# Reordering the seams between chained products of a four-layer diffusion backbone on one NeuronCore

## What is computed

```
mod = silu(cond) @ w_mod[i] + b_mod[i]
h = rms_norm(x, g_pre) * (1 + scale) + shift
out = product(s) of the sub-layer on h
x = x + gate * rms_norm(out, g_post)
```

## Time and profile before

| | |
|---|---|
| median of 3 runs | 2044.71 us (2044.56 to 2045.04) |
| profiled execution | 2046.58 us, of which span 2044.8 us |
| TensorE clock granted, mean | 0.976 |
| busy: PE, DVE, ACT, POOL | 1935.7, 1191.7, 924.0, 713.5 us |
| DMA | 324.29 MB, 44.6% of 16 engines in the main queue |

### The profile page before, as it was taken

How to read it: one execution, slowest core, us unless ns; L and a number is a source line. 1 busy time by engine, 2 the same in 40 slices (tenths; PEclk the granted TensorE clock), 3 DMA queues, 4 the chain that set the end, 5 groups by cost and what they waited for, 6 DMA issues and landing times.

```text
span 2044.8 us, 29870 instructions
## 1 busy us (share of the span) xinstructions
PE 1935.7 (95%) x11679; PEld 1713.0 (84%) x11679; DVE 1191.7 (58%) x1789; ACT 924.0 (45%) x1566; POOL 713.5 (35%) x515
## 2 busy tenths in 40 slices
PE   6699999999998989999999998899999979899998
PEld 3589998799996767999987956899987867799986
DVE  3557761566626675777615844777724684777722
ACT  3444442554546645444424325544424444544422
POOL 0223324333335553333344722333343521333342
PEclk8799999999999989999999999999999989899999
DMA  9764346433330137533374655533365413333342
GB/s 399 319 247 135 124 164 246 169 123 124 97 134 27 48 134 305 187 125 125 116 246 172 207 155 202 211 124 124 113 240 182 174 40 114 112 128 124 124 132 72
DMA packets 80316, 324.29 MB, mean 159 GB/s; under 512 B 9009, under 2 KB 17713, under 8 KB 66609
## 3 DMA queue, kind: packets, MB, share of 16 engines
q1 hardware_dynamic: 78496, 319.42, 44.6%
q10 hardware_dynamic: 1680, 2.96, 0.4%
HBM read 317.24 MB, written 5.10 MB: 158 GB/s over the span
## 4 chain that ended last, share of the span: by engine, by line
PE 81%; DVE 7%; ACT 5%; issue 3%; POOL 2%; DMA 2%; SPq 0%; DVEq 0%; ACTq 0%; POOLq 0%
PE pair L1825 18%; PE pair L1827 17%; PE pair L1826 17%; PE pair L1861 7%; PE pair L1862 7%; PE pair L1863 7%; DVE x L1333 2%; PE pair L1982 2%; PE pair L2076 1%; DMA raw<-in_pool 1%; ACT junk L908 1%; PE pair L1796 1%; DVE wk L1324 1%; PE pair L1987 1%; PE pair L2203 1%
## 5 line engine op out<-in xcount | busy, mean ns | idle before, releaser
L752 POOL TENSOR_TENSOR w_lo<-raw,w_hi 128x512 fp32r<-128x512 f32 (+1 forms) x375 | 587.8, 1569 | 1133.2 <-ACT w_hi L880 1133.1
L1825 PE MATMUL pair<-h_hi,w_hi 128*128 128x386 f32 (+1 forms) x2008 | 687.5, 342 | 13.2 <-POOL h_lo L759 10.5
L1827 PE MATMUL pair<-h_hi,w_lo 128*128 128x386 f32 (+1 forms) x2008 | 682.6, 340 | 0.0
L1826 PE MATMUL pair<-h_lo,w_hi 128*128 128x386 f32 (+1 forms) x2008 | 682.0, 340 | 0.0
L1267 DVE TENSOR_TENSOR w_lo<-raw,w_hi 128x512 fp32r<-128x512 f32 x339 | 411.3, 1216 | 325.5 <-ACT w_hi L880 325.4
L880 ACT ACTIVATE w_hi<-raw 128x1024 fp32r<-128x1024 f32 x375 | 392.9, 1050 | 292.6 <-PE pair L1863 225.6
L1825 PEld LDWEIGHTS pair<-h_hi,w_hi 128*128 128x128 f32 (+1 forms) x2008 | 380.0, 189 | 22.2 <-POOL h_lo L759 16.7
L1826 PEld LDWEIGHTS pair<-h_lo,w_hi 128*128 128x128 f32 (+1 forms) x2008 | 380.5, 189 | 0.9
L1827 PEld LDWEIGHTS pair<-h_hi,w_lo 128*128 128x128 f32 (+1 forms) x2008 | 380.0, 189 | 0.3
L1416 DVE SCALAR_TENSOR_TENSOR acc<-pair,taps,acc 128x385 f32<-128x385 f32 x176 | 108.9, 619 | 207.4 <-ACT acc L984 207.4
L984 ACT ACTIVATE acc<-pair,taps 128x386 f32<-128x386 f32 x176 | 117.3, 666 | 224.7 <-PE pair L1827 224.7
(11 more groups left out here) (286 smaller groups left out, 2128.0 us busy)
## 6 DMA issues: line engine op xcount, KB each, us to landing
raw<-in_ffn_in SPq DMA_DIRECT2D x176, 512.0 KB, 3.5
raw<-in_ffn_out SPq DMA_DIRECT2D x88, 512.0 KB, 3.5
mod_raw<-in_w_mod SPq DMA_DIRECT2D x36, 1024.0 KB, 6.8
mod_base<-in_w_mod SPq DMA_DIRECT2D x31, 1024.0 KB, 7.1
mod_more<-in_w_mod SPq DMA_DIRECT2D x18, 1024.0 KB, 20.4
raw<-in_ssd_conv SPq DMA_DIRECT2D x32, 512.0 KB, 3.5
raw<-in_ssd_z SPq DMA_DIRECT2D x16, 512.0 KB, 3.5
raw<-in_ssd_out SPq DMA_DIRECT2D x16, 512.0 KB, 3.8
```

What stands on the lines that cost most here:

```text
L752: pool.tensor_tensor(w_lo[:, m % SLOTS, 0:w], raw[:, m % SLOTS, 0:w], w_hi[:, m % SLOTS, 0:w].bitcast(F32), ALU.subtract).then_inc(w_low_p ...
L1825: ten.matmul(to, wh, h_hi[:, k, cols], start=k == 0, stop=False, skip_group_check=True)
L1826: ten.matmul(to, wh, h_lo[:, k, cols], start=False, stop=False, skip_group_check=True)
L1827: ins = ten.matmul(to, wl, h_hi[:, k, cols], start=False, stop=k == KD - 1, skip_group_check=True)
```

## The change

1. `FILLS` for 12 pieces goes from (3, 7) to (1, 6): 1, 5 and 6 pieces in place of 3, 4 and 5.
2. In `transition`, ACT rounds chunk n only after `unit_high(t, 1)`, and chunk n+1 after `unit_high(t, 2)` with the others. `unit_high(t, 0)` now comes before `first(t, 2)`, and `unit_stage(t, 1)` before `second(t, 2)`.
3. POOL does the low part of unit 0 alone, before any weight part. DVE does all 1024 columns of unit 1, and both halves of unit 2. DVE makes the low part of chunk n after `unit_stage(t, 2)`.
4. `unit_high(t, 2)` is two copies of 512 columns, of which the first doesn't wait for DVE's part of the stage. DVE's `unit_low(t, 2)` is two subtractions.
5. PE's `in_start` waits for the first half of unit 2; the second half is waited for inside the first tile, before k = 4.
6. Seam 0 keeps the orders of ACT and DVE, but takes 3 to 5, with POOL's new order.

```diff
-FILLS = {12: (3, 7), 4: (1, 3)}
+FILLS = {12: (1, 6), 4: (1, 3)}
+        def highs_made(t, c, half=1):
+            return 4 * t + c + 1 + (half if c == 2 else 0)
+        def lows_on_dve(t, c, half=1):
+            return 4 * t + c + 1 + (half if c == 2 else 0)
+        def lows_on_pool(t):
+            return t + 1
+        def stage_free(engine, e):
+            if e >= 2:
+                t, c = divmod(e - 2, 3)
+                engine.wait_ge(h_lo_pool, lows_on_pool(t))
+                engine.wait_ge(h_lo_dve, lows_on_dve(t, c))
...
             def transition(t, n):            # POOL
-                low_to(n + 1)
                 unit_low(t, 0)
-                unit_low(t, 1)
-                low_to(n + 2)
-                unit_low(t, 2)
                 low_to(n + 4)
...
             def unit_high(t, c):             # ACT
                 act.wait_ge(stage_act, e + 1)
-                act.wait_ge(stage_dve, e + 1)
-                act.activation(h_hi[:, :, cols], stage[:, e % 2, :, :], ACT.Copy).then_inc(h_hi_ready, 1)
+                if c < 2:
...
+                else:
+                    for half in range(2):
+                        ks = slice(4 * half, 4 * half + 4)
+                        if half:
+                            act.wait_ge(stage_dve, e + 1)
+                        act.activation(h_hi[:, ks, cols], stage[:, e % 2, ks, :], ACT.Copy).then_inc(h_hi_ready, 1)
...
                 first(t, 1)                  # ACT, transition
-                round_to(n + 1)
                 unit_stage(t, 0)
                 second(t, 1)
+                unit_high(t, 0)
                 first(t, 2)
-                unit_high(t, 0)
+                unit_stage(t, 1)
                 second(t, 2)
-                unit_stage(t, 1)
                 unit_high(t, 1)
-                round_to(n + 2)
+                round_to(n + 1)
                 unit_stage(t, 2)
                 unit_high(t, 2)
                 round_to(n + 4)
...
             def unit_low(t, c):              # DVE
+                for half in range(2) if c == 2 else (1,):
+                    ks = slice(0, KD) if c == 1 else slice(4 * half, 4 * half + 4)
+                    vec.wait_ge(h_hi_ready, highs_made(t, c, half))
+                    vec.tensor_tensor(h_lo[:, ks, cols], stage[:, e % 2, ks, :], h_hi[:, ks, cols].bitcast(F32),
+                                      ALU.subtract).then_inc(h_lo_dve, 1)
...
                 unit(t, 1)                   # DVE, transition
-                low_to(n + 1)
                 weigh(t, 2)
                 residual(t, 2)
+                unit_stage(t, 1)
                 unit_low(t, 0)
-                unit_stage(t, 1)
                 unit(t, 2)
                 unit_low(t, 1)
-                low_to(n + 2)
                 unit_stage(t, 2)
+                low_to(n + 1)
                 unit_low(t, 2)
                 low_to(n + 4)
...
             def tile(to, n, w, cols, behind=None):      # PE
                 for k in range(KD):
+                    if behind is not None and k == 4:
+                        ten.wait_ge(h_lo_dve, lows_on_dve(behind, 2, 1))
...
             def in_start(t):
-                for c in range(3):
-                    unit_there(t, c)
+                ten.wait_ge(h_lo_pool, lows_on_pool(t))
+                ten.wait_ge(h_lo_dve, lows_on_dve(t, 2, 0))
```

More of the change, by code:

```diff
@@ L635, in scan_traffic @@
                     else:
-                        sp.wait_ge(h_lo_dve, event(1, 2) + 1)
+                        sp.wait_ge(h_lo_dve, lows_on_dve(1, 2))
                         sp.wait_ge(mod_used, end_pieces(1)[-1] + 1)
@@ L757, in unit_low @@
                 e, cols = event(t, c), slice(AT[c], AT[c] + P)
-                pool.wait_ge(h_hi_ready, e + 1)
+                pool.wait_ge(h_hi_ready, highs_made(t, c))
                 pool.tensor_tensor(h_lo[:, 0:4, cols], stage[:, e % 2, 0:4, :], h_hi[:, 0:4, cols].bitcast(F32),
@@ L916, in unit_stage @@
                 act.wait_ge(mod_done, vector_done(l, SHIFT1 if part else SHIFT0))
-                if e >= 2:
-                    act.wait_ge(h_lo_pool, e - 1)
-                    act.wait_ge(h_lo_dve, e - 1)
+                stage_free(act, e)
                 for k in range(4):
@@ L928, in unit_high @@
                 act.wait_ge(stage_act, e + 1)
-                act.wait_ge(stage_dve, e + 1)
-                act.activation(h_hi[:, :, cols], stage[:, e % 2, :, :], ACT.Copy).then_inc(h_hi_ready, 1)
+                if c < 2:
+                    act.wait_ge(stage_dve, e + 1)
+                    act.activation(h_hi[:, :, cols], stage[:, e % 2, :, :], ACT.Copy).then_inc(h_hi_ready, 1)
+                else:
+                    for half in range(2):
+                        ks = slice(4 * half, 4 * half + 4)
+                        if half:
+                            act.wait_ge(stage_dve, e + 1)
+                        act.activation(h_hi[:, ks, cols], stage[:, e % 2, ks, :], ACT.Copy).then_inc(h_hi_ready, 1)
             def transition0(n):
@@ L1347, in unit_stage @@
                 vec.wait_ge(mod_done, vector_done(l, SHIFT1 if part else SHIFT0))
-                if e >= 2:
-                    vec.wait_ge(h_lo_pool, e - 1)
-                    vec.wait_ge(h_lo_dve, e - 1)
+                stage_free(vec, e)
                 for k in range(4, KD):
@@ L1358, in unit_low @@
                 e, cols = event(t, c), slice(AT[c], AT[c] + P)
-                vec.wait_ge(h_hi_ready, e + 1)
-                vec.tensor_tensor(h_lo[:, 4:, cols], stage[:, e % 2, 4:, :], h_hi[:, 4:, cols].bitcast(F32),
-                                  ALU.subtract).then_inc(h_lo_dve, 1)
+                for half in range(2) if c == 2 else (1,):
[3 more added lines that the diff above has]
+                                      ALU.subtract).then_inc(h_lo_dve, 1)
             def transition0(n):
@@ L1820, in turn_unit, with tile @@
                         ins.then_inc(unit_turned, 1)
-            def tile(to, n, w, cols):
+            def tile(to, n, w, cols, behind=None):
                 for k in range(KD):
+                    if behind is not None and k == 4:
+                        ten.wait_ge(h_lo_dve, lows_on_dve(behind, 2, 1))
                     wh, wl = (v[:, n % SLOTS, k * w:(k + 1) * w] for v in (w_hi, w_lo))
@@ L1828, in tile @@
                 return ins
-            def unit_there(t, c):
-                ten.wait_ge(h_lo_pool, event(t, c) + 1)
-                ten.wait_ge(h_lo_dve, event(t, c) + 1)
             def fill(t, first, last):
@@ L1849, in in_tile @@
                 chunk_ready(s.n0 + j)
-                tile(tile_bank(j)[:, 0:COLS], s.n0 + j, P, slice(0, COLS)).then_inc(w_used, 1)
+                tile(tile_bank(j)[:, 0:COLS], s.n0 + j, P, slice(0, COLS), t if j == 0 else None).then_inc(w_used, 1)
                 if j == 3:
```

## The result

| | before | after |
|---|---|---|
| median, 4 runs each | 2044.88 us (2044.56 to 2046.06) | 2023.86 us (2018.22 to 2025.00) |
| ratio, 95% interval | | 0.9891 (0.9872 to 0.9909) |
| profiled execution, span | 2046.58, 2044.8 us | 2018.22, 2016.5 us |

21.0 us faster by the medians, where 21.2 was forecast; by the ratio, taken over all runs, it is 22.3, and its interval reaches from 18.6 to 26.2 us. An agreement to 0.2 us is closer than four runs can tell.

What follows compares the result with a forecast made beforehand. PE's matmuls were taken as the bound (PE busy 95%), so only its idle time and lower clock could give time. Seam gains plus clock terms, less 0.5 for loads, summed to 21.2 us: 2044.71 to 2023.5, range 2018 to 2031.5.

Steps and rivals of the forecast that it cites:

- two clock terms: Time lost to PE's lower clock in the tiles behind seams 2 and 6: 1.6 and 1.3 us regained.
- the loads: Loads of the last two modulation pieces, issued about 1 us later: 0.5 us lost in all.
- seam 4: Chain counts in full: turn of unit 2 from 1286.11 to 1283.7, first tile from 1294.10 to 1290.1; gain 4.0 us.
- seam 6: With 4 pieces, `h` ends last: first tile 4.2 to 5.0 us after the turn of unit 2; gain 4.3 us.
- (a): Seam 1, before unit 2's turn: POOL's weight part leaves, `residual` of unit 1 1.04 us shorter, cover for (b) only.
- (b): Seam 1: DVE's weight part leaves the place before `weigh` of unit 2, which comes 0.29 us earlier.
- (c): Seam 1: POOL's low part of unit 0 stops nothing, so `residual` of unit 2 drops from 1.96 to 1.29: 0.67 us.
- the rival on the clock: Clock falls in every seam, about 8 us lost each, against 18.4 gained without clock terms: slower, 2068 us; chance 0.05.
- From the turn to the tile: Seam 1, unit 2's turn to first tile: turn 1.0, pieces 4.5 and 0.9; tile at 401.2 against 403.76.
- locked tail: Rival: POOL's part of chunk n stops DVE twice before the first tile; gain only 9 to 18 us; chance 0.14.
- The rule: DVE and POOL exclude each other as whole instructions; in seam 6's tail that would take some 1.3 us off the sum.
- a gain given back by the weights: Rival: tiles behind a seam are paced by weights, not PE, and wait; time stays 2044.7 us; chance 0.04.

Runs made afterwards that it cites:

- e8: Changed kernel with ScalarE's old order of unit 0's copy, `first(t, 2)`, unit 1's stage and `second(t, 2)`, weight parts staying late; 2027.74 us, ratio 0.9920.
- e3: Changed kernel with the weight parts of chunk n back in the middle of the chain on ScalarE, POOL and DVE; 2027.60 us, ratio 0.9915.
- e5: Changed kernel with unit 2 copied and subtracted whole, the first tile waiting for all of it; 2024.61 us, ratio 0.9904.
- e4: Kernel before, with one move: POOL makes its part of chunk n after the low part of unit 0; 2045.30 us, ratio 1.0005.
- e9: Changed kernel with ScalarE's copy of chunk n alone back in the middle, so POOL's part follows its low part of unit 0; 2020.66 us, ratio 0.9893.
- e1: Kernel before, with only the pieces moved from (3, 7) to (1, 6); 2043.58 us, ratio 0.9991.
- e7: As e6, with DVE also making unit 0's low part after unit 2's scaling; 2016.87 us, ratio 0.9864 to the kernel before.
- e6: As e2, with the pieces at (3, 8) in seam 4; 2018.24 us, ratio 0.9871 to the kernel before.
- e0_same_again: Changed kernel run and profiled again without edit; 2022.37 us, ratio 0.9888 to the kernel before.
- e2: Changed kernel with the pieces at (3, 7) as before, so the new orders alone; 2022.11 us, ratio 0.9884 to the kernel before.

## Why the prediction was right

- *What bounds the seams.* "What the change can take is PE's idle time there, and the time lost to a lower clock": the sum by seams was 18.8 without clock, and 18.6 and 17.8 were measured. With the two clock terms, less the loads, 21.2 against 21.0 in the medians. That the total is so close is luck in part: seam 4 gave 1.3 to 1.4 us less than forecast, seam 6 0.6 to 1.0 more, seam 0 some 1 us where nothing was forecast, and the clock terms came out at 4.1 and 2.2 for 2.9.
- *Steps (a) to (c).* Each shows as said. (a) 2.33 became 1.29. The room that it left was worth nothing by itself in seam 1, but ScalarE's copy of unit 0 found place in it, before the end of the product. (b), (c): the turn was said to be 394.8 - 387.57 = 7.2 after the product's last matmul, and is 7.08. e8 shows that (c) is the carrying step: 0.9 us of `residual` in seam 1, and with 0.2 for the earlier stage of unit 1, which comes back with it, 1.1 in each seam. The weight parts, (a) and (b), add to that in seams 3 to 5, where the end of the product gives no cover or too little of it: this is what e8 leaves there, and in e3, which puts both back at once, the turns of seams 3 to 5 are 1.6 to 1.9 later and the others 0.8 to 1.0. In the working, 0.29 + 0.67 is 0.96, not 0.97, and the 18.4 of the rival on the clock should be 18.3; neither matters.
- *From the turn to the tile.* 8.5 of the 18.6 us lie here: the weight parts and POOL's low parts of units 1 and 2 have left this path. e5 prices the halves alone (1.2 us in seam 6). No run puts the low parts back on POOL, so for the rest the cause is read from the rows and not shown by an experiment.
- *Cover in the tail.* 2.2 us were worked out for seam 1; with the same 0.5 for the start, 2.3 are there. The locked tail didn't come: POOL and DVE met (POOL's part took 1.52 for 1.30), but DVE's two low parts kept their 1.22 and 0.64 in seam 1. In seam 3 the pair took 1.57 for 1.28, in cover.
- *The rule.* The Trainium skill's lock, "SBUF — State Buffer", section "SBUF: two separate sides", by which an instruction of one engine holds the ports that the two share until it ends, agrees with the pairs of rows here: `residual` takes 1.28 alone, 2.17 when POOL's 1.19 began 0.11 before, and DVE's low part 2.87 for 0.68 in e4. That its price comes from where two instructions meet, and not from how many there are, the counts show too: DVE has 7 instructions more and makes more of `h_lo`, and yet its busy time fell from 1191.7 to 1187.8 us.
- *Seam 4 was mis-sized:* "the turn goes from 1286.11 to 1283.7 ... at full clock a turn and six pieces are 6.4". The turn came as said (10.48 after the product, 10.7 forecast), but behind it the clock was low and the stretch took 7.97: 2.7 us gained, not 4.0. The step that was off is "at full clock": it took a shorter wait to leave the clock up. After a wait of 2.25, with 1.29 before the turn of unit 1, the clock fell in both profiles of the changed kernel, and in e5 and e9 as well; after 2.32 in e1 (with 2.25 before the turn of unit 1) and 1.65 in e7 it didn't, after 1.89 in e6 it did. So a length of wait doesn't settle it, and what does isn't shown by these runs.
- *Seam 6 made up for it:* 4.9 and 5.3 for 4.3, since the tail from turn to tile is 4.2 and 3.8 us, at and below the low end of 4.2 to 5.0. Its clock term, half of 2.7 taken, was 2.6 in one profile and 0.7 in the other. Over all profiles the 15 steps behind seam 6 took 10.6 to 10.8 us in the three with the old orders, and in the nine with the new ones 8.0 to 8.1 in three and 9.6 to 10.0 in six.
- *The clock term of seam 2* came out (9.58 to 8.08 us, 1.6 forecast), but its reason isn't shown. In e4, whose waits there are 1.82 and 2.49 us, the 15 steps took 8.03. So the idle time doesn't decide it, and the loss behind seam 2 stands in one profile of twelve.
- *Seam 0 was put at nothing* because PE had no wait there. But the low parts came just as late as PE's pieces. The change brought them forward, and where the pieces ran faster too, the first tile came 1.2 and 1.1 us sooner after the turn (`e0_same_again` above).
- *Not seen as a loss:* that (1, 6) takes 0.9 us in seam 4 and 0.6 each in seams 2 and 3. I had costed the orders and the pieces together. Alone they are 24 and 2 us (the 2 hardly told from nothing), and the rows of e2, e6 and e7 show that the pieces belong elsewhere.

Nothing speaks for the rival of a slower clock in all seams, nor for that of a gain given back by the weights. Between the seams, the clock terms left out, the first profile after is 2.0 us shorter in all than the one before, and the second 0.2.

## What to carry to other kernels

- When two engines lock each other, moving one instruction only moves the meeting. Write down both engines' times around the critical instruction, and find for the other engine a stretch in which the first waits anyway; here it was the 1.35 us just behind the product's last matmul, in which DVE waits for ScalarE's square, and one earlier copy on a third engine was enough to reach it.
- Where an engine must do a fixed amount of work between two products, its idle time, and the clock behind it, is the whole prize. Filler work earns nothing by being elsewhere, as long as the chain beside it sets the end; once the chain is shorter, the filler belongs in front of the longest wait that is left.
- A wait that is cut short may still leave the clock low behind it. Cost the work behind a wait at both levels.

## What I had not expected

- The start of the kernel varies by up to 3.6 us from profile to profile (first tile of seam 0 at 94.2 to 97.8), of which up to 2.9 stand before the third turn of seam 0; one broadcast load there takes 8.8 to 11.3 us to land. A single profile can't be compared over the whole span to better than that.
- A lock costs by the other engine's instruction, not by one's own: in seam 2 of the kernel before, a DVE product of one column (L1330) took 1.20 us beside POOL, and 0.16 without:

```profile
802.44 1.20 DVE L1330 TENSOR_TENSOR inv<-inv,ssd_inv 128x1 f32<-128x1 f32 x1
```
- The clock behind a seam can't be read off the wait before it: the steps behind seam 2 ran at full clock after 1.62 us in `e1_fills_alone` and after 2.49 in `e4_pool_part_later`, and not after 2.57 in the kernel before.
